# The 512-column float32r matmuls stream their columns in pairs from the two halves in turn

## What is computed

```python
h = rms_norm(x, norm1_gain[l]) * (1.0 + sc1) + sh1
z = h @ w_in[l]
...
x = x + gt1 * (merged @ w_out[l])
h2 = rms_norm(x, norm2_gain[l]) * (1.0 + sc2) + sh2
x = x + gt2 * ((jax.nn.silu(h2 @ ffn_w_gate[l]) * (h2 @ ffn_w_up[l])) @ ffn_w_down[l])
...
for layer in range(DEPTH_2):
    qkv = h @ w_in[layer]
    ...
    x = x + mix @ w_out[layer]
    u = h @ w_up
    ...
    return (jax.nn.silu(gate) * val) @ w_down
```

## Time and profile before

| | us |
|---|---|
| two timed runs | 2309.75 and 2311.57, median 2310.66 |
| span of the profiled execution | 2308.2 |
| PE busy | 2253.8 |
| PEld busy | 1799.2 |
| POOL busy | 1393.4 |
| DVE busy | 947.8 |
| ACT busy | 612.0 |
| moved by DMA | 206.08 MB, 89 GB/s over the span |

### The profile page before, as it was taken

The page is one execution under the profiler, slowest core; times in us unless marked ns, Lnnn a source line. Parts: engine busy times, 40 slices in busy tenths (PEclk is TensorE's granted clock), DMA queues, the critical chain, the costliest instruction groups (busy, mean ns, idle before and its releaser), DMA issues.

```text
span 2308.2 us, 28721 instructions
## 1 busy us (share of the span) xinstructions
PE 2253.8 (98%) x10597; PEld 1799.2 (78%) x10597; DVE 947.8 (41%) x1742; ACT 612.0 (27%) x1335; POOL 1393.4 (60%) x522
## 2 busy tenths in 40 slices
PE   7999999999999999999999999999999999999997
PEld 5787887787888888787787788888787787888885
DVE  6744777544110132325636433302235627433202
ACT  3263652112111100104643222201015623222200
POOL 4755404776777777774018777777773038777773
PEclk9999999999999999999999999999999999999999
DMA  8322103422222232222002222222221012222221
GB/s 327 128 74 92 56 20 114 176 80 75 103 91 91 96 146 109 92 91 73 1 19 73 105 95 91 92 91 91 91 91 55 1 37 74 94 101 96 91 91 55
DMA packets 32725, 206.08 MB, mean 89 GB/s; under 512 B 4080, under 2 KB 4336, under 8 KB 11632
## 3 DMA queue, kind: packets, MB, share of 16 engines
q1 hardware_dynamic: 32192, 200.27, 24.1%
q10 hardware_dynamic: 432, 4.46, 0.5%
HBM read 202.61 MB, written 2.10 MB: 89 GB/s over the span
## 4 chain that ended last, share of the span: by engine, by line
PE 92%; DVE 3%; POOL 1%; issue 1%; ACT 1%; DMA 0%; DVEq 0%; ACTq 0%; SPq 0%; POOLq 0%
PE PS L756 25%; PE PS L758 25%; PE PS L757 25%; PE PS L1052 5%; PE PS L1078 4%; PE PS L1067 2%; PE PS L1025 1%; PE PS L828 1%; PE PS L770 1%; POOL w_hi L426 1%; POOL w_lo L430 1%; PE PS L1108 1%; DVE ring L1997 1%; PE PS L1337 0%; DMA xT<-xT_dram 0%
## 5 line engine op out<-in xcount | busy, mean ns | idle before, releaser
L426 POOL TENSOR_TENSOR w_hi<-raw,zero_c 128x2048 fp32r<-128x2048 f32 (+1 forms) x238 | 593.7, 2508 | 834.0 <-PE PS L758 832.7
L430 POOL TENSOR_TENSOR w_lo<-raw,w_hi 128x2048 fp32r<-128x2048 f32 (+1 forms) x238 | 757.4, 3197 | 12.4
L756 PE MATMUL PS<-f_hi,w_hi 128*128 128x512 f32 x992 | 393.5, 397 | 2.1 <-POOL w_lo L430 1.4
L758 PE MATMUL PS<-f_hi,w_lo 128*128 128x512 f32 x992 | 393.3, 396 | 0.0
L757 PE MATMUL PS<-f_lo,w_hi 128*128 128x512 f32 x992 | 393.2, 396 | 0.0
L756 PEld LDWEIGHTS PS<-f_hi,w_hi 128*128 128x128 f32 x992 | 186.8, 188 | 48.8 <-POOL w_lo L430 2.3
L758 PEld LDWEIGHTS PS<-f_hi,w_lo 128*128 128x128 f32 x992 | 186.8, 188 | 45.6
L757 PEld LDWEIGHTS PS<-f_lo,w_hi 128*128 128x128 f32 x992 | 186.8, 188 | 45.3
L756 PE MATMUL PS<-a_hi,w_hi 128*128 (+1 forms) x528 | 209.7, 397 | 0.0
L757 PE MATMUL PS<-a_lo,w_hi 128*128 (+1 forms) x528 | 209.3, 396 | 0.0
L758 PE MATMUL PS<-a_hi,w_lo 128*128 (+1 forms) x528 | 209.3, 396 | 0.0
(11 more groups left out here) (424 smaller groups left out, 3692.4 us busy)
## 6 DMA issues: line engine op xcount, KB each, us to landing
raw<-slabs_dram SPq DMA_DIRECT2D x161, 1024.0 KB, 4.8
aux<-ada_dram SPq DMA_DIRECT2D x18, 512.0 KB, 5.1
ada_first<-ada_dram SPq DMA_DIRECT2D x11, 512.0 KB, 14.1
cmpw<-cmpw_dram ACTq DMA_DIRECT2D x2, 2048.0 KB, 11.6
ada_late<-ada_dram SPq DMA_DIRECT2D x8, 512.0 KB, 3.3
ada_last<-ada_dram SPq DMA_DIRECT2D x8, 512.0 KB, 6.1
xT<-xT_dram SPq DMA_DIRECT2D x1, 2048.0 KB, 9.1
out_dram<-t SPq DMA_DIRECT2D x4, 512.0 KB, 2.7
```

The source lines that it names most:

```text
L426: high = nc.gpsimd.tensor_tensor(w_hi[:, slot, c], raw[:, slot, c], zero[:, 0:c.stop - c.start], ALU.add)
L430: low = nc.gpsimd.tensor_tensor(w_lo[:, slot, c], raw[:, slot, c], w_hi[:, slot, c].bitcast(f32), ALU.subtract)
L756: nc.tensor.matmul(out, a_hi_, b_hi_, start=start, stop=False)
L758: return nc.tensor.matmul(out, a_lo_, b_hi_, start=False, stop=stop)
```

## The change

The helper `three` gets a local function `woven`. Where the last dimension of an operand has 512 elements it is read as 2 halves (h) x 128 (c) x 2 neighbours (e), and passed in the order c, h, e: words 0, 1, then 256, 257, then 2, 3, then 258, 259, and so on. The output and both streamed operands get the same order, so each column still lands at its own place in the bank, and the sums are the same. The stationary operands `a_hi_`, `a_lo_` are untouched. Calls with 384 or 312 columns are not changed.

```diff
             def three(out, a_hi_, a_lo_, b_hi_, b_lo_, start, stop):
+                def woven(x):
+                    return x.rearrange("p (h c e) -> p c h e", h=2, e=2) if x.shape[-1] == 512 else x
+                out, b_hi_, b_lo_ = woven(out), woven(b_hi_), woven(b_lo_)
                 nc.tensor.matmul(out, a_hi_, b_hi_, start=start, stop=False)
                 nc.tensor.matmul(out, a_hi_, b_lo_, start=False, stop=False)
                 return nc.tensor.matmul(out, a_lo_, b_hi_, start=False, stop=stop)
```

## The result

The changed kernel takes 3057.69 us, the median of two runs (3050.72 and 3064.66), against 2310.66 us. The ratio is 1.323, with a 95% interval of 1.320 to 1.327: a third slower. The profiled execution has a span of 3062.8 us, 754.6 us more than before. 754.6 us / 7488 matmuls = 100.8 ns for each 512-column matmul, where the prediction took 0.

A forecast was written before the change was run, and what follows sets the result against it. The prediction took TensorE's 512-column matmuls in `three` to bound the kernel, 76% of the span. The 2308.2 us span plus 0 for the change, with timed runs 2.5 us above the span, gave 2310 us, range 2165 to 2480 us.

The forecast's parts named there:

- The count: Matmuls of `three` with 512 columns: 156 slabs x 16 = 2496 calls, 7488 matmuls.
- the 234.0 ns: Mean distance from one start to the next of the 512-column matmuls of `three`, before the change.
- the share of the chain: Three matmul lines of `three` in the chain that ended last: 7488 x 234.0 ns = 1752 us, 76% of the span.
- the loss would arrive whole: Whole kernel: if matmuls became slower, every other engine has more room, so the full loss reaches the end.
- It makes zero the value I take: 512-column matmuls of `three`: the broken pattern changes their time by 0, taken with weak support.
- VectorE's short runs: Line 1971 on VectorE: 128 elements in runs of 4 or of 8 both take 0.28 us.
- In pairs every second column still lies beside the one before it: Streamed operand of the changed matmuls: neighbouring words stay together in twos, offered as support for a change of zero.
- The surplus seen above counts columns: Matmuls of `three`: 20 ns above 213.3 at 512 columns, read as pauses of about 6.7 ns; the change leaves them alone.
- Both bounds of the sum: 512-column matmuls: lowest 215.6 ns each, -138 us; highest 429 ns, the float32 rate, +1460 us.
- the half-rate rival: 512-column streams: a fetch serves four neighbouring words, so pairs halve the rate; 429 ns, 3770 us; chance 0.20, or worse.
- The pauses go: 512-column matmuls: alternating between two places 1 KB apart avoids the pauses; -138 us, 2172 us; chance 0.27, wholly or in part.
- The pauses double: 512-column matmuls: half the useful words per fetched group, 20.7 ns more each; +155 us, 2465 us; moderate loss, chance 0.15.

The follow-up runs named there:

- eight eighths: Against the kernel before, read only: single words streamed in turn from eight eighths of the 512 columns, in the second layer's up part; 487 ns per matmul.
- singles: Against the kernel before: streamed words taken singly from two halves in turn, ScalarE and VectorE writing them in a row; 2198.21 us, ratio 0.9514.

## Why the prediction was wrong

The count, the 234.0 ns and the share of the chain held; so did the 7.5 us for each ns (754.6 us for 100.8 ns) and "the loss would arrive whole". The shapes that were to keep their steps kept them (173, 144 and 429 ns), and GpSimd's wait moved by 48 steps, as said.

The step that failed is "It makes zero the value I take", the price of the broken stream, where 101 ns were measured, all or nearly all of them on the read of SBUF (3032 us with the read broken alone, 2310.55 with the write). It rested on three supports. VectorE's short runs cost nothing, but its 128 words in 0.28 us ask for a word every 2 ns, and TensorE for more than two per ns; the row was the nearest and still no evidence. "In pairs every second column still lies beside the one before it" was the second: pairs cost 327 ns all the same, while single words from two places, no column beside the one before it, take 216. "The surplus seen above counts columns" was the third: 18 of the same 20 ns go when the stream reads one group again and again, without a column less. Both bounds of the sum were drawn from other streams, and the upper one, the 429 ns of the float32 rows, is none: every second word takes 453 ns and eight eighths 487. Had I read the surplus as a stream that is already short of its memory, the half-rate rival would have weighed more than 0.20, since nothing in the rows spoke for zero at that rate.

The rivals. *The pauses go*: wrong for this change, but the surplus was there to be won (singles, 216 ns, and 2198 us reached of its 2172). I had bound it to "returning alternately to two places", which is true for single words and false for pairs. *The pauses double*: 20.7 ns, a fifth of the measured price. *Half rate*: the right side, and of the rivals the nearest in kind, a fetch that serves neighbouring words, which the table fits and doesn't prove; its size was off, 195 ns for 101, since the stream falls to about two thirds of a column per cycle (213.3 of 327 ns) and not to one half. No row before had a broken stream from which two thirds could have been read. The interval left this rival out by design, and between 2480 and 3770 us, where the result lies, I had put nothing.

Of the two sentences that the prediction weighed, both about contiguous patterns: the warning of the Trainium skill, "PSUM — Partial Sum Buffer", Specifications, put the cost in PSUM, and the run that breaks only the write, in pairs, shows none (0.9999). The Trainium skill, "Advanced Engine Details and Errata", Memory Cachelines, lets pairs pass in PSUM, and there the run agrees; for SBUF it asks for two hits on a 16-byte line, which the pairs give, and at this rate they were not enough: 327 to 347 ns for 234. The measurement decides in both.

## What to carry to other kernels

Where a float32r stream sets the pace, break neither its run nor its neighbourhood: two words of a place are too few (once the places are 32 bytes apart or more), four nearly enough, and a step of two words costs double. Single words from exactly two places are the exception and beat a run in a row by 8% per matmul, if the order can be had for nothing, as from the host, or by engines that write in a row and take from PSUM. No run here tries this with another data type. And where a price has no row, the middle between two bounds is not a safe place to leave empty.

## What the runs showed that I had not expected

- The streamed read of SBUF is sensitive to order, and the write to PSUM, in pairs, is not: 3032 us for the one, 2310.5 us for the other.
- A float32r matmul of 512 columns takes 216 ns in some orders of its stream and 234 ns for a run in a row: 18 ns of it come from what is read, and not from the number of columns.
- Pairs 8 and 16 bytes apart are free (217, 218 ns), 24 bytes cost 243, and from 32 bytes on the step is 327 ns at most distances, with some phases at 333 to 350 that don't go by the distance.
- Words two apart take 453 ns on TensorE. VectorE and ScalarE take them from PSUM without loss (692 and 598 ns), and from SBUF with some (1235 for 1032, 955 for 709 ns).
- Single words from two places go at 216 ns at any distance tried from 8 bytes to 1 KB, from four at 284, from eight at 487. Open is what makes every second word so much dearer than this, and why the step of pairs varies by phase between 327 and 347 ns.
